# Seven block products of eight in the up-projection of an encoder's feed-forward, which is split into an up phase and a down phase

## The reference

```python
def conv_ffn(x, w_up, conv_w, conv_b, w_down):
    hid = dwconv_centred(x @ w_up, conv_w, conv_b)
    gate, val = jnp.split(hid, 2, axis=-1)
    return (jax.nn.silu(gate) * val) @ w_down
...
        x = x + y @ w_out[l]
        x = x + conv_ffn(rmsnorm(x, ffn_norm_gain[l]), ffn_w_up[l], ffn_conv_w[l],
                         ffn_conv_b[l], ffn_w_down[l])
```

## Time and profile before

| what | value |
|---|---|
| median of 3 runs (lowest to highest) | 2605.91 us (2605.62 to 2606.47) |
| the profiled execution's own time | 2607.4 us |
| its span, first to last instruction | 2605.6 us |
| mean granted TensorE clock | 0.994 of full speed |
| PE, matmuls | 2551.5 us busy, 13362 of them |
| DVE, ACT, POOL busy | 1404.4, 894.1, 807.9 us |
| transfers | 204.66 MB, mean 79 GB/s |

### The profile page before, as it was taken

One profiled execution on the slowest core, in us unless ns is written; L12 is line 12 of the kernel. 1 busy time (PEld: TensorE's weight loads), 2 busy tenths in 40 slices (PEclk: granted clock), 3 DMA queues, 4 the chain that ended last, 5 costly groups with the idle time before them and its releaser, 6 DMA issues.

```text
span 2605.6 us, 33332 instructions
## 1 busy us (share of the span) xinstructions
PE 2551.5 (98%) x13362; PEld 2165.9 (83%) x13362; DVE 1404.4 (54%) x1629; ACT 894.1 (34%) x1540; POOL 807.9 (31%) x446
## 2 busy tenths in 40 slices
PE   7999999999999999999999999999999999999999
PEld 6989998788888888888788899887888888888887
DVE  3476558546444444444656755674564444444445
ACT  4335658413221122222234365692232222222221
POOL 3232114143333333333323411251333333333331
PEclk9999999999999999999999999998999999999999
DMA  4433444111111111111123344422111111111111
GB/s 153 129 121 122 149 137 138 71 57 41 49 49 49 49 49 49 49 49 49 62 98 97 98 145 146 158 96 81 49 49 49 49 49 49 49 49 43 47 49 73
DMA packets 72045, 204.66 MB, mean 79 GB/s; under 512 B 5816, under 2 KB 28344, under 8 KB 70456
## 3 DMA queue, kind: packets, MB, share of 16 engines
q1 hardware_dynamic: 51848, 178.13, 20.7%
q10 hardware_dynamic: 20056, 24.51, 3.1%
HBM read 175.32 MB, written 27.30 MB: 78 GB/s over the span
## 4 chain that ended last, share of the span: by engine, by line
PE 88%; DVE 5%; ACT 3%; issue 1%; DMA 1%; POOL 0%; SPq 0%; ACTq 0%; DVEq 0%; POOLq 0%
PE PS L548 23%; PE PS L552 23%; PE PS L551 23%; PE PS L632 3%; PE PS L636 3%; PE PS L635 3%; PE PS L802 2%; PE PS L791 2%; PE PS L973 1%; PE PS L938 1%; PE PS L781 1%; ACT LG L1289 1%; PE PS L780 1%; DVE CV L1687 1%; ACT PTX L1296 1%
## 5 line engine op out<-in xcount | busy, mean ns | idle before, releaser
L497 POOL CAST WH<-RAW 128x1024 fp32r<-128x1024 f32 x192 | 237.6, 1238 | 1661.7 <-PE PS L548 1099.2
L548 PE MATMUL PS<-HH,WH 128*128 128x512 f32 x1904 | 747.7, 393 | 0.0
L551 PE MATMUL PS<-HL,WH 128*128 128x512 f32 x1904 | 744.6, 391 | 0.0
L552 PE MATMUL PS<-HH,WL 128*128 128x512 f32 x1904 | 744.5, 391 | 0.0
L499 POOL TENSOR_TENSOR WL<-RAW,WH 128x1024 fp32r<-128x1024 f32 x192 | 495.0, 2578 | 15.4
L1948 DVE TENSOR_TENSOR X<-PS,X 128x512 f32<-128x512 f32 x384 | 258.9, 688 | 374.6 <-PE PS L552 374.2
L552 PEld LDWEIGHTS PS<-HH,WL 128*128 128x128 f32 x1904 | 357.4, 188 | 80.0
L548 PEld LDWEIGHTS PS<-HH,WH 128*128 128x128 f32 x1904 | 357.8, 188 | 77.9
L551 PEld LDWEIGHTS PS<-HL,WH 128*128 128x128 f32 x1904 | 357.7, 188 | 77.1
L1442 ACT ACTIVATE FPAD<-PS 128x512 f32<-128x512 f32 x176 | 102.7, 596 | 884.4 <-PE PS L552 884.4
L1966 DVE SCALAR_TENSOR_TENSOR CVV<-FPAD,PARM,CVV 128x1024 f32<-128x1024 f32 x44 | 95.3, 2166 | 377.8 <-ACT CVV L1448 377.8
(11 more groups left out here) (227 smaller groups left out, 3106.5 us busy)
## 6 DMA issues: line engine op xcount, KB each, us to landing
RAW<-wst SPq DMA_DIRECT2D x192, 512.0 KB, 3.5
TOE<-toe_d SPq DMA_DIRECT2D x64, 512.0 KB, 3.8
XBS<-xbc_d SPq DMA_DIRECT2D x24, 512.0 KB, 4.3
xbc_d<-CV ACTq DMA_DIRECT2D x16, 512.0 KB, 4.0
tok_d<-ST ACTq DMA_DIRECT2D x12, 512.0 KB, 3.4
ZG<-tok_d SPq DMA_DIRECT2D x16, 384.0 KB, 3.5
toe_d<-row_d SPq DMA_DIRECT2D x4, 1024.0 KB, 12.9
X<-xT SPq DMA_DIRECT2D x2, 2048.0 KB, 7.9
```

The lines of the kernel that those rows point to most:

```text
L497: nc.gpsimd.tensor_copy(hi, raw).then_inc(hi_done, 1)
L548: ins = nc.tensor.matmul(out, wh, xh, start=first, stop=False)
L551: nc.tensor.matmul(out, wh, xl, start=False, stop=False)
L552: return nc.tensor.matmul(out, wl, xh, start=False, stop=last)
```

## The change

**Up phase.** The first two up units of a layer (gate and value of group 0) stay as they are. For each of the other 20, the weight unit (1024 x 256) is seen as two by two blocks (512 features x 128 channels), and the input as two by two blocks (512 features x 512 tokens). The four blocks of the result come from seven block products (Strassen's method in Winograd's form), each 4 x 3 matmuls of 512 columns (`product`, `seven`): 84 in a unit. Before that, DVE makes four sums and differences of the input's blocks, in place in X (`combo`), and ACT and DVE split them into high and low parts (T2H, T1H, and over parts of HH, HL and X). Per unit, POOL makes four combinations of weight blocks (S1 to S4) and all seven low parts, ACT the seven high parts, into a ring of eight places of 512 columns in WH and WL (`combined`, `cast`). ACT copies the first product out of PSUM to QS (`first_copy`) and DVE adds the products together in five additions. The convolution's outer taps now read PSUM directly; FPAD is gone. A unit of weights comes in one transfer of 1 MB, into RAW or RAWB. Every gated group is stored to HBM (`act_store`, 1 MB).

**Down phase.** It follows the up phase and runs over the tokens' halves: 11 pairs of channel tiles each, 48 matmuls in a pair, accumulated over all 22 channel tiles in eight PSUM banks. Activations are loaded back (`act_load`, 256 KB each) into a ring of four pairs and split there by ACT (`high`) and DVE (`low`). The down weights are loaded and split twice, once per half. X is added once per tile, 16 additions in all, from `xmid`, a copy of X made in HBM before the normalisation, which now scales X in place.

**Counts.** PE has 480 matmuls of 128x512 fewer, 240 per layer, and its other matmuls are the same in number and shape.

```diff
         def _(pool):
...
+            def combined(l, s):
+                n = l * SU + s
+                a11, a12, a21, a22 = quarters(s)
+                s1, s2, s3 = (TMP[:, i].rearrange("p (k n) -> p k n", k=4) for i in range(3))
+                TT = nc.gpsimd.tensor_tensor
+                pool.wait_ge(sr_full[s % 2], 16 * (n // 2 + 1))
+                TT(s1, a21, a22, ALU.add).then_inc(sa_done, 1)
+                pool.wait_ge(sa_done, 4 * n + 1)
+                TT(s2, s1, a11, ALU.subtract).then_inc(sa_done, 1)
+                TT(s3, a11, a21, ALU.subtract).then_inc(sa_done, 1)
+                def low(i, t):
+                    pool.wait_ge(sh_done, n * PR + i + 1)
+                    return TT(ring(WL, s * PR + i), t, ring(WH, s * PR + i).bitcast(F32), ALU.subtract
+                              ).then_inc(sw_ready, 1)
...
         def _(pe):
...
-                def up(g, unit, s, part):
-                    columns_unit(l, unit, s, a0 + A_UP + g * 8 + part * 4, True)
...
+                def product(s, i, x, b, first):
+                    n = l * SU + s
+                    pe.wait_ge(sw_ready, n * PR + i + 1)
+                    if i == 4:
+                        pe.wait_ge(first_copied, n + 1)
+                    if i > 4:
+                        pe.wait_ge(su_done, n * 3 + i - 3)
...
+                    for k in range(4):
+                        last = mm3(bank(b), (wh[:, k], wl[:, k]), (xh[:, k], xl[:, k]), first and k == 0, k == 3,
+                                   onto=not first)
+                    last.then_inc(sp_done, 1)
...
+                def seven(s):
+                    b = 4 * (s % 2)
+                    pe.wait_ge(f_conv, 2 * (l * 2 * NG + s) + 2)
+                    product(s, 0, normed(0, 0), b, True)
...
+                    product(s, 1, (T2H, quad(XL, 0, 0)), b + 3, True)
...
+                    product(s, 2, (T1H, quad(XL, 0, 1)), b + 1, True)
...
+                    product(s, 3, (quad(HH, 0, 1), quad(XL, 1, 1)), b + 2, True)
+                    product(s, 4, normed(1, 0), b, False)
+                    product(s, 5, normed(1, 1), b + 1, False)
...
+                    product(s, 6, (quad(HL, 0, 1), quad(XL, 1, 0)), b + 2, False)
...
+                def pair(th, d, order, before=()):
...
+                        xh, xl = AR[:, RING[i % 8], 0], AR[:, RING[i % 8], 1]
+                        last = mm3(bank(dt), wtile(s, kk * 1024 + dt * P), (xh, xl), first and kk == 0,
+                                   d == NG - 1 and kk == 1, w_used if j == 0 else None)
...
+                        elif d == 0 and l + 1 < DEPTH:
+                            pair(th, d, [(kk, dt) for kk in range(2) for dt in range(KT - 1)] + [(0, KT - 1), (1, KT - 1)],
+                                 ((4, lambda: norm_spread(n, 0)), (9, lambda: norm_back(n, 0))))
...
         def _(act):
...
+                def cast(v, i):
+                    s = v - STD
+                    n = l * SU + s
+                    j = s * PR + i
+                    if j < 8:
+                        act.wait_ge(cb_ready, 2 * v0 + (2 if j < 4 else 4))
+                    else:
+                        act.wait_ge(sp_done, l * SU * PR + j - 7)
...
+                def first_copy(v):
+                    n = l * SU + v - STD
+                    act.wait_ge(sp_done, n * PR + 1)
+                    act.wait_ge(cb_ready, 2 * (v0 + v))
+                    A(QS[:], bank(4 * (v % 2)), ACT.Copy).then_inc(first_copied, 1)
...
+                if l + 1 < DEPTH:
+                    act.wait_ge(f_gate, 2 * (l + 1) * NG)
+                    act.dma_start(PARM[:], params[l + 1]).then_inc(par_in, 16)
+                    nc.scalar.preload_act_table(ACT.Sqrt)
+                for d in range(1, NG + 3):
+                    high(d)
...
         def _(dve):
...
+                for v in range(STD, 2 * NG):
+                    n, b = l * SU + v - STD, 4 * (v % 2)
+                    if v % 2 == 0:
+                        gated(v // 2 - 1, 0)
+                        gated(v // 2 - 1, 1)
+                    dve.wait_ge(sp_done, n * PR + 2)
+                    dve.wait_ge(first_copied, n + 1)
+                    TT(QS[:], QS[:], bank(b + 3), ALU.add).then_inc(su_done, 1)
...
+                    TT(UU[:], QS[:], bank(b + 1), ALU.add).then_inc(su_done, 1)
...
+                    TT(bank(b + 3), UU[:], bank(b + 2), ALU.add).then_inc(su_done, 1)
+                    dve.wait_ge(sp_done, n * PR + 6)
+                    TT(bank(b + 1), QS[:], bank(b + 1), ALU.add).then_inc(cb_ready, 1)
+                    if v == 2 * NG - 1:
+                        low(0)
+                    dve.wait_ge(sp_done, n * PR + 7)
+                    TT(bank(b + 2), QS[:], bank(b + 2), ALU.add).then_inc(cb_ready, 1)
+                    conv(v, 0)
+                    conv(v, 1)
```

More of the change, by code:

```diff
@@ L138, in then @@
         self.k += 1
[L139 to L142 removed]
+        self.eng.wait_ge(self.sem, self.k)
 def trunk(nc, xT, xtok, wst, params, consts, onehot, lnrow, table, outT):
@@ L370, in dt_weights, with ring, quarters, quad @@
             return w[:, 0:W_AT[1]].rearrange("p (k n) -> p k n", k=KT)[:, :, UC:UC + DTW]
+        def ring(w, j):
+            return w[:, ring_at(j):ring_at(j) + HALF].rearrange("p (k n) -> p k n", k=4)
+        def quarters(s):
+            raw = (RAW, RAWB)[s % 2][:].rearrange("p h (k c n) -> p h k c n", k=4, c=2)
+            return raw[:, 0, :, 0], raw[:, 1, :, 0], raw[:, 0, :, 1], raw[:, 1, :, 1]
+        def quad(t, k, th):
+            return t[:, 4 * k:4 * k + 4, half(th)]
+        def taps(v, ct):
+            at = PAR["ffn_conv"][0] + (v % 2 * FT + ct) * 4 + v // 2 * 8
+            return [PARM[:, at + i:at + i + 1] for i in range(4)]
+        def hidden(v, ct):
+            return bank(4 * (v % 2) + 2 * ct, 2)
         def per_head(t, w=HD):
@@ new lines, in _ @@
+                A(T1H[:], quad(X, 0, 1), ACT.Copy).then_inc(th_done, 1)
+                tap(0, 0)
+                tap(0, 1)
+                silu(0, 0)
+                silu(0, 1)
+                for i in range(4):
+                    cast(STD, i)
+                tap(1, 0)
+                tap(1, 1)
+                act.wait_ge(cb_ready, 2 * v0 + 4)
+                act.wait_ge(tc_done, l * 4 + 4)
+                A(quad(HH, 0, 1), quad(X, 1, 1), ACT.Copy).then_inc(th_done, 1)
+                cast(STD, 4)
@@ new lines, in _ @@
+                cast(STD, 5)
+                A(quad(HL, 0, 1), quad(X, 1, 0), ACT.Copy).then_inc(th_done, 1)
+                cast(STD, 6)
+                for v in range(STD, 2 * NG):
+                    g, more = v // 2, v + 1 < 2 * NG
+                    if more:
+                        cast(v + 1, 0)
+                    first_copy(v)
+                    if more:
+                        cast(v + 1, 1)
+                    for i in range(2, 6 if more else 2):
+                        cast(v + 1, i)
+                    if not more:
+                        high(0)
+                    tap(v, 0)
+                    if more:
+                        cast(v + 1, 6)
+                    tap(v, 1)
+                    if v % 2 == 0:
+                        silu(g, 0)
+                        silu(g, 1)
@@ L2023, in _, with add_down @@
-                low(g, 1)
-                step.end()
-                for i in range(8, 16):
-                    add(i, n0)
-                n0 = b0 + B_FILLS - 16
+                def add_down(i):
+                    th, dt = divmod(i, KT)
+                    dve.wait_ge(b_full, b0 + 4 * OUT_U + i + 1)
+                    if dt == 0:
+                        dve.wait_ge(x_back[th], 32 * (l + 1))
+                    x = X[:, dt, half(th)]
+                    TT(x, bank(dt), x, ALU.add).then_inc(b_free, 1)
```

695 lines of the change are left out of this document (386 added, 309 removed).

## The result

The changed kernel takes 2516.11 us (median of 4 runs, 2512.27 to 2516.7), the kernel before 2605.76 us beside it: ratio 0.9653, 95% interval 0.9636 to 0.967. That is about 90 us less, where the forecast had 120.6 less (2485 us). The time lies 1.1 us above the range. The profiled execution took 2516.7 us, with a span of 2514.9 us and a mean granted clock of 0.990 (0.994 before).

A forecast was written before the change was run, and what follows sets the result against it. PE, busy 98% of the span, was taken to bound the kernel. 123.6 us less matmul work, less 3.0 us of net waits, gave 120.6 us less: median 2485 us, range 2474 to 2515.

The forecast's parts named there:

- PE's work, 123.6 us less: Both layers' feed-forward: fewer matmuls, and product units at 0.2267 us per matmul on one address grid; 61.8 us less per layer.
- Steady units, nothing lost: Product units of the up phase: POOL, DVE and ACT fit beside PE's 19.06 us per unit; stall put at nothing.
- Rivals 1, 2 and 3: Grid does nothing for new addresses, 2498.5 us, chance 0.17; DVE chain misses the product, 2529, 0.15; POOL becomes bound, 2730, 0.04.
- Rival 2: Product units: taps held by POOL make the chain through DVE late for PE; 44 us, so 2529; chance 0.15.
- First product unit: First product unit of each layer: DVE's block sums, low parts and gatings 0 to 2.2 us late; 2 us in all.
- Start of the down phase: Layer 0: second pair's high parts stand on ACT behind the last gating and a table load; 1.4 us.
- the transfers are 1.5 MB: Down phase: data transferred during a pair of 11 us, listed among the work that must fit beside PE.
- Rival 4: Down phase: weights and activations come late for its pairs, half a us for each of 44; 2507 us; chance 0.04.
- End of half 0: Layer 0: DVE's additions and sums stand behind the low parts of pair 13; 1.6 to 6 us, taken as 4.
- Normalisation: Before the feed-forward: HL made from two SBUF operands while POOL works; 0 to 2 us per layer, taken as 1.
- Boundary: Layer boundary: the sum of half 1 is left as a wait; 0 to 4 us, taken as 1.
- The old 7.4 us: PE's feed-forward waits before the change, for HL, ACC and X; most were expected to go, subtracted from the new waits.

The follow-up runs named there:

- eight products: Changed kernel with the second product of each of the 20 units per layer issued twice, so 96 matmuls per unit again; 2615.98 us, ratio 1.0033.
- the two address runs: Changed kernel with slot-0 product weights shifted 64 bytes off the grid, 2526.52 us; kernel before with second AHI and ALO moved onto HH's grid, 2600.95 us.
- gating early: Changed kernel with group 0's first gating on DVE ahead of the last two low parts, the second behind the first three additions; 2505.93 us, ratio 0.9614.
- the two smaller orders: Changed kernel with the last sum before two low parts at the normalisation, and the second pair's high parts before the last gating's wait; 2513.26 us, ratio 0.964.

## Why the prediction was right and wrong

- **PE's work, 123.6 us less: right.** 19.04 us per product unit against 19.06; pairs of 10.90 and 11.10 against 10.89 and 11.07, which is 0.9 us over all 44 pairs, as much as the units gained. With eight products each added matmul costs its 0.2267 us again, and the two address runs show the share of the grid.
- **Steady units, nothing lost: right.** Rivals 1, 2 and 3 fell. Rival 2's held taps did not come: they are no longer operations with two SBUF operands.
- **First product unit, "0 to 2.2 us late", 1 us per layer: wrong**, 3.5 us per layer and about 5 to 6 with the clock. The prices were near: low parts of 2048 columns at 2.4 us took 2.29 three times and 3.40 once, the two gatings 4.51 against 4.36. What my count left out is that DVE's work is not in one piece: it stands idle for 4.30 and 2.23 us, waiting for ACT, ahead of them.
- **Start of the down phase, 1.4 us for AR: right**, 1.8. But **"the transfers are 1.5 MB"** per pair left out the return of X, two transfers of 2 MB per layer on the same queue. The waits for WL, 6.0 us in the profiled execution, come from it. Rival 4 had named the mechanism with a price for every pair; it was the third and fourth pair of each layer alone.
- **End of half 0, 1.6 to 6 us, taken as 4: wrong in size**, 7.5 us and over 2 us of low clock. The additions and sums took 13.1 us together, where I had 13.0. But the low parts ahead of them were done 8.3 us into the pair, not at "5 to 7": the first began at 4.6 us, and both were held, 3.83 us for two.
- **Normalisation 1 us per layer: near**, 1.3. The held operations are HL's, as forecast (1.65 us at 580.62, where 0.68 is the shortest), but the recorded wait is for ACC, the sum that stands behind them; for HL itself PE only pauses three times for 0.2 to 0.3 us, about 1 us more in each layer.
- **Boundary 1 us: too low**, 2.4, and the clock fell there too (0.83 in 1280 to 1290 us). The old 7.4 us went as forecast.
- **What a wait costs: missing.** Each was counted at its own length. Mean clock 0.994 to 0.990, some 10 us.

Waits were forecast at 10.4 us new, and were 27.3: 17 us. The profiled execution was forecast at 2486.8 us and took 2516.7, so 29.9 are to be found. Beside the 17 there are up to 10 us of clock, the 2 us of pauses for HL, and, as an estimate, 2 to 3 us by which a wait costs more than is recorded for it: from the matmul at 1037.73 to the one at 1040.38 are 2.65 us for a wait of 2.26, where 0.23 is normal, and the next matmul comes 0.1 us late; there are eleven such places. Outside the feed-forward nothing was lost in sum: PE reached the first matmul of L922 at 191.03 us in place of 194.41 (L780 before), and lost 1.8 us in the rest of layer 0's mixers, where a wait for HL (L1138) is 2.90 us in place of 0.73, and 0.4 in layer 1's. Together that is about 30 us, with a clock figure that is no better than a few us.

So the step that failed is the last term of the sum, the waits (+3.0 us in all, +10.4 of them new): the new waits were 27.3 us, because DVE's idle time ahead of the first product unit, the return of X on SP's queue and the held low parts at the end of half 0 were left out or priced too low; and what the lower clock costs behind a wait was no term at all. My own criterion, "PE's waits in the feed-forward are over 15 us together", was met. The price of the seams was wrong, while PE's work and the steady units were right.

## What to carry to other kernels

When a change shortens the engine that bounds, the steady loop may follow it exactly and the gain still leak at the seams: list, for each seam, every instruction ahead of the one that is waited for, on its engine and on its DMA queue, with what each must wait for itself, and with the longest duration seen and not the mean. Put work that nobody waits for (here a gating, 4 MB of X, low parts for a later pair) behind the one that releases PE; three such moves brought 24 us. Then add to the long waits what PE pays at the lower clock afterwards.

## What the hardware showed that I had not expected

- After a wait of 3.48 us PE ran 12 matmuls at 0.43 us, the 1.2 GHz level, before it was back at 0.227. After 7.50 us it was 11 matmuls. In layer 1, after the same 3.48 us, it was six. After the waits of 1.76, 2.26 and 1.34 us at the start of the down phase it did not fall (1.00 in the 10 us behind each), after 1.32 us at the normalisation it fell in layer 0 (0.83 in 580 to 590 us) and not in layer 1 (1.00 in 1834 to 1844). After 2.40 us at the layer boundary it fell (0.83 in 1280 to 1290), after 2.63 us for WL in the run of the two smaller orders it did not (1.00 in 1051 to 1061). So in these runs the length of the wait alone does not decide. Filling the wait (eight products) or removing it (gating early) kept the clock at 1.00.
- Where weights and inputs lie decides the pace of a 128x512 fp32r matmul: 0.2267 us with both on one grid, 0.2302 on average with half of the weights 64 bytes off.
- POOL's hold more than doubles a DVE subtraction of 512 columns, 1575 ns against 694.
